# Output stages with a 512-column and a 256-column product per weight tile, and ScalarE's rounding of weights moved ahead

## The chip, the core and the metric

The kernel runs on one core of a Trainium2 chip. The metric is the device time of one execution in microseconds (us). TensorE (PE in the profile) multiplies matrices, VectorE (DVE) and ScalarE (ACT) work on rows of 128 partitions, GpSimd (POOL) does small odds and ends here, and SyncE (SP) issues most of the DMAs.

## The reference, cut to what matters

Two transformer-like blocks run one after the other on 256 tokens of width 2048, all in float32.

```
first block:  h = rms_norm(x); proj = h @ w_in            # 2048 x 8192
              y = [gated short convolution, causal attention], each normalised and gated
              x = x + y @ w_out                            # 2048 x 2048, first output stage
second block: modulation = silu(c) @ w_ada + b_ada        # 2048 x 12288, for c and c_ctx
              q, k, v, u = modulate(rms_norm(x)) @ w_in_2; k, v also of the context rows
              mix = [window attention with context keys, multi-scale pooling of u]
              x = x + g_a * (mix @ w_out_2)                # 2048 x 2048, second output stage
              x = x + g_m * (relu(modulate(rms_norm(x)) @ w_up)^2 @ w_down)   # 8192 wide
              rms_norm(x)
```

Products must be more exact than one pass in the reduced float32 format of TensorE gives, so each factor is split in a rounded part ("hi") and the rest ("lo"), and three products are summed: hi*hi, lo*hi and hi*lo. The fourth, lo*lo, is left out in both kernels.

## The kernel before, in words

**Units.** All large products are cut into units. A unit makes 128 output features for 256 tokens, from 16 weight tiles of 128x128. Its weights come in two halves of 8 tiles (128x1024 float32, 512 KB each). There are 248 units: 64 for the first projection, 16 for the first output stage (`U_OUT1`), 8 for keys and values (`U_KV`), 16 for queries and pooling (`U_Q`, `U_POOL`), 16 for the second output stage (`U_OUT2`), and 128 for the MLP in four groups of 16 up units and 16 down units.

**A half on its way.** SP loads it into one of 4 slots of `raw` (`weight`, L256), after VectorE has finished with what the slot held. ScalarE rounds it into `hi` (`split`, L757, the copy is recorded at L755) once the data are there and TensorE has used the half four places earlier (`w_used`). VectorE subtracts to get `lo` (`split`, L1090, recorded at L1088, since the helper `tt` has its call there) and signals `lo_done`. The four slots hold two units, so both engines prepare unit j+2 in the turn that belongs to unit j.

**TensorE.** `unit` (L402) calls `half_unit` twice. Each half waits for its own `lo_done`, and then issues three matmuls of 256 columns for each tile: hi by the activations' hi half (L396), lo by their hi half (L397), hi by their lo half (L398). All add into the first 256 columns of one PSUM bank, `G0` or `G1` by turns. A unit may begin when VectorE or ScalarE has emptied the unit two places earlier (`evac_done`). `pair_unit` (L413), which only the down units of the MLP use, issues two matmuls for each tile: hi by both activation halves at once, 512 columns into the full bank (L422), and lo by the hi half, 256 columns into the first half of the bank (L423). It waits for both weight halves before its first matmul. The bank then holds two parts, and VectorE must add both.

**The first output stage.** For unit j VectorE goes through `out_lap` (L1354): the lo part of unit j+2's first half, the addition of the bank to `resid` (L1362, recorded at L1088), two operations that make a tile of the modulated context (L1364, L1365), the lo part of unit j+2's second half, the lo part of the context tile (`actC`), and the addition of squares. ScalarE goes through `out_body` (L937): hi of the first half, hi of the context tile (which waits for L1365), the square of `resid`, and only then hi of the second half. One row of the modulation product (four groups of narrow matmuls, `ada_rows`, L438) stands between the two halves of each unit on TensorE; SP loads these rows (1 MB each) in its own order between the weights, and waits for an earlier row to be used first. The key and value units that follow read all 16 context tiles in order.

**The second output stage.** For unit j VectorE takes lo of the first half, multiplies the bank by the gate and adds it to `resid` (L1521), takes lo of the second half, makes the lo part of the MLP's input (L1525, which waits for ScalarE's hi part, L946) and adds squares. ScalarE takes hi of the first half, L946 (which waits for L1521), the square, and hi of the second half. The sum of squares gates the MLP's normalisation (`total_sums`, L467).

Of the kernel before, what the change touches and what calls it, by code (L numbers as in the profile page):

```python
# [7 lines left out]
ALU = mybir.AluOpType  # L8
# [7 lines left out]
T = 256  # L16
D = 2048
KT = D // P
# [6 lines left out]
UNITS_IN, UNITS_OUT = 64, 16  # L25
# [3 lines left out]
U_OUT1 = UNITS_IN  # L29
# [13 lines left out]
for _name, _n in (("gain1", 16), ("conv_w", 24), ("conv_gain", 8), ("attn_gain", 8), ("q_gain", 1), ("k_gain", 1),  # L43
# [13 lines left out]
    "act up": {"relu_done": 2, "nt_hi": 2, "hi_done": 4},  # L57
    "act down": {"hi_done": 4},
    "act last down": {"hi_done": 4, "sqs": 2, "sq_ready": 2},
    "dve w_out": {"seq": 4, "nt_ready": 4, "lo_done": 8, "nt": 4, "inC": 4, "sqs": 4, "sq_added": 4},  # L60
    "dve q": {"p_turned": 4, "p_copied2": 4, "rot": 2, "seq": 14, "rope_done": 2, "qr_ready": 2, "nt": 2, "inB": 2, "scores": 8, "negmax_ready": 2, "lo_done": 4, "tile": 2, "probs_scaled": 8},
    "dve w_out_2": {"lo_done": 8, "sqs": 4, "sq_added": 4, "x_hi": 4, "inA": 4},
    "dve up": {"relu_done": 2, "seq": 2, "lo_done": 4, "nt": 2, "inB": 2},
# [40 lines left out]
def program(nc, t_in, out):  # L104
    with ExitStack() as ctx:
# [275 lines left out]
        def _(pe):  # L381
# [20 lines left out]
            def unit(at, j, x, ready=None, ready_base=0, ada=None):  # L402
                half_unit(at, j, 0, x, ready, ready_base)
                if ada is not None:
                    if ada % KT == 0 and ada > 0:
                        ada_turn()
                    else:
                        ada_rows(ada)
                half_unit(at, j, 1, x, ready, ready_base)
                if ada is not None and ada % KT == 0 and ada > 0:  # L410
                    ada_rows(ada)
# [38 lines left out]
            def part_sums(n):  # L450

                pe.wait_ge(ada_taken, 4 * (n + 1))
                if n:
                    pe.wait_ge(part_added, n)
                for m in range(4):
                    x = pe.matmul(PART[:, m:m + 1], part[:, m * P:(m + 1) * P], ones[:, 0:1], start=(m == 0), stop=(m == 3),
                                  skip_group_check=True)
                x.then_inc(part_summed, 1)
# [89 lines left out]
                conv_body(HEADS + h)  # L548
            broadcast()
            for n in range(UNITS_OUT):  # L550
                unit(At(U_OUT1), n, actB, inB, ada=2 * KT + n)
                if n == 1:
                    part_sums(7)

            def total_sums(n):

# [146 lines left out]
            tile_values(1)  # L703
            tiles_of(bank, (7,)).then_inc(w_used, 1)
            tiles_of(bank, (8, 9), last=True).then_inc(w_used, 1)
            unit(at, 1, actB)
            with turn.lap(pe, (UNITS_OUT - 2) // 2, "pe w_out_2") as i:
                for j in range(2):
                    unit(At(U_OUT2 + 2, 2, i), j, actB)

            def up_unit(at, j):
                half_unit(at, j, 0, actU, extra=2)
# [34 lines left out]
        def _(act):  # L747
# [9 lines left out]
            def split(at, j, half=1):  # L757

                slot = (2 * j + half) % RING
                act.wait_ge(raw_full[slot], at.loads(j, half) * 16)  # L760
                act.wait_ge(w_used, at.unit(j, 1 + half, 2))
                copy(hi[:, slot], raw[:, slot]).then_inc(hi_done, 1)
                own(hi_done)
# [173 lines left out]
            def out_body(at, i, ctx_too):  # L937

                for j in range(4):
                    u = slice(i * 4 + j, i * 4 + j + 1) if isinstance(i, int) else bass.ds(i * 4 + j, 1)  # L940
                    split(at, j, 0)
                    if ctx_too:
                        high(actC[:, u, 0:T], t4[:, 3:4])
                    if not ctx_too:
                        evacuated(at, j)
                        act.activation(actU[:, u, 0:T], resid[:, u], ACT.Copy, scale=scale_m[:, u]).then_inc(x_hi, 1)  # L946
                        own(x_hi)
                    square(at, j, (sq[:, j % 2:j % 2 + 1], resid[:, u]))
                    split(at, j)

            with turn.lap(act, 4, "act w_out") as i:
                out_body(At(U_OUT1, 4, i), i, True)
# [118 lines left out]
        def _(dve):  # L1071
# [3 lines left out]
            def own(event):  # L1075

                dve.wait_ge(event, turn.next(event.name))
# [9 lines left out]
            def tt(dst, a, b, op):  # L1087
                return dve.tensor_tensor(dst, a, b, op)  # L1088

            def split(at, j, half=1):  # L1090

                slot = (2 * j + half) % RING
                dve.wait_ge(hi_done, at.unit(j, 5 + half, 2))
                tt(lo[:, slot], raw[:, slot], hi[:, slot], ALU.subtract).then_inc(lo_done, 1)
                own(lo_done)

            def summed(at, j):

                dve.wait_ge(w_used, at.unit(j, 2, 2))
                dve.wait_ge(evac_done, at.unit(j))  # L1100
                return G[j % 2][:, 0:T].rearrange("p (a t) -> p a t", a=1)

            def evacuated(at, j):
                dve.wait_ge(evac_done, at.unit(j, 1))
# [233 lines left out]
            def add_squares(s):  # L1338
                dve.wait_ge(sq_ready, turn.next("sqs") + 2 * HEADS + CONV_TILES)
                tt(sqsum[:], sqsum[:], sq[:, s], ALU.add).then_inc(sq_added, 1)  # L1340
                own(sq_added)
# [12 lines left out]
            def out_lap(at, i, first=False):  # L1354
                for j in range(4):
                    u = bass.ds(i * 4 + j, 1) if not isinstance(i, int) else slice(i * 4 + j, i * 4 + j + 1)
                    split(at, j, 0)
                    if j == 0 and first:
                        modulation_ready()
                    if j == 2 and first:  # L1360
                        part_add(7)
                    tt(resid[:, u], resid[:, u], summed(at, j), ALU.add).then_inc(evac_done, 1)  # L1362
                    dve.wait_ge(ctx_full[j], i * 16 + 16)
                    seq(dve.scalar_tensor_tensor(t4[:, 2:3], ctx_raw[:, j:j + 1], scale_a[:, 1, u], CTX_BC3, ALU.mult, ALU.mult))  # L1364
                    dve.tensor_scalar(t4[:, 3:4], t4[:, 2:3], adav[:, 1, u], None,  # L1365
                                      ALU.add).then_inc(nt_ready, 1)
                    own(nt_ready)
                    split(at, j)
                    low(actC[:, u, 0:T], actC[:, u, T:2 * T], t4[:, 3:4], inC)
                    add_squares(j % 2)  # L1370
# [142 lines left out]
            turn.base["inA"] = 2 * KT - turn.local.get("inA", 0)  # L1513


            with turn.lap(dve, 4, "dve w_out_2") as i:
                at = At(U_OUT2, 4, i)
                for j in range(4):
                    u = bass.ds(i * 4 + j, 1)
                    split(at, j, 0)  # L1520
                    dve.scalar_tensor_tensor(resid[:, u], summed(at, j), adav[:, 0, bass.ds(i * 4 + G_A + j, 1)],  # L1521
                                             resid[:, u], ALU.mult, ALU.add).then_inc(evac_done, 1)
                    split(at, j)
                    dve.wait_ge(x_hi, turn.next("x_hi"))
                    dve.scalar_tensor_tensor(actU[:, u, T + 2:], resid[:, u], scale_m[:, u], actU[:, u, 0:T], ALU.mult,  # L1525
                                             ALU.subtract).then_inc(inA, 1)
                    own(inA)
                    add_squares(j % 2)
            take_sums(ss[:, 8:10], SUMS[:, 0:2], add=False)
            dve.wait_ge(sum_taken, turn.value("sum"))  # L1530
            mean_square(ss[:, 8:10], D)
# [162 lines left out]
```

## Time and profile before

| what | us |
|---|---|
| three timed runs | 1774.19, 1772.69, 1773.1; median 1773.1 |
| the profiled execution, its own time | 1774.28 |
| its span in the profile | 1772.4 |
| busy: TensorE, VectorE, ScalarE | 1635.3, 1165.5, 768.3 |

The span runs from the first to the last instruction. 1.9 us of the execution's own time lie outside it. Busy times overlap, so they don't add up to the span. TensorE's matmuls are pipelined: in a row of the timeline the number after the start is how long one matmul takes from start to end, while the distance of two starts is what it costs in the stream.

### The profile page before, as it was taken

What the parts mean: (1) busy time and instruction counts of PE and PEld (TensorE: products, weight loads), DVE (VectorE), ACT (ScalarE), POOL (GpSimd) and SP (SyncE); (2) the same over time, 40 slices, a digit from 0 to 9 for tenths busy, and PEclk for the clock granted to TensorE, in tenths of its full rate; (3) what the DMA queues carried; (4) which work ended last, traced back from release to release, by engine and by line L of the source; (5) the groups of instructions that cost most, each with busy time, mean ns of one, the idle gap of its engine ahead of it and who ended that gap; (6) DMA issues with size and microseconds to landing.
All of it is one profiled execution on the core that took longest, in us unless ns stands there. A gap on an engine that the chain in (4) does not pass through costs nothing.

```text
span 1772.4 us, 33734 instructions
## 1 busy us (share of the span) xinstructions
PE 1635.3 (92%) x12254; PEld 1501.3 (85%) x12254; DVE 1165.5 (66%) x1798; ACT 768.3 (43%) x1067; POOL 32.0 (2%) x49
## 2 busy tenths in 40 slices
PE   3799999899969977998989889999999999999996
PEld 3799998799968867877878879989998999899985
DVE  4577776688885557576755566656665666566675
ACT  4344443344433334444434445434543454345542
POOL 0000000000000000000000010000000000000000
PEclk9899999899989999999999989999999999999998
DMA  7688787688848765762224445555555556555552
GB/s 298 245 277 293 282 289 243 233 318 334 318 169 323 277 242 186 296 254 92 76 84 152 147 151 184 185 188 189 180 188 189 188 179 187 189 184 186 180 190 92
DMA packets 88120, 374.74 MB, mean 211 GB/s; under 512 B 9985, under 2 KB 10513, under 8 KB 75233
## 3 DMA queue, kind: packets, MB, share of 16 engines
q1 hardware_dynamic: 82224, 335.97, 55.3%
q10 hardware_dynamic: 4608, 33.56, 5.2%
q0 software_dynamic: 1200, 4.02, 0.7%
q8 instruction: 60, 0.98, 0.2%
q14 instruction: 28, 0.22, 0.0%
HBM read 371.40 MB, written 2.10 MB: 211 GB/s over the span
## 4 chain that ended last, share of the span: by engine, by line
issue 71%; DVE 12%; PE 11%; ACT 5%; DVEq 1%; POOL 0%; ACTq 0%; POOLq 0%
DVE lo L1088 5%; ACT hi L755 2%; PE G L396 2%; PE G L397 2%; PE G L398 2%; PE ADA L438 1%; PE M L636 1%; ACT sq L934 1%; DVE sqsum L1088 1%; DVE blk L1088 1%; PE S L610 1%; DVE sm L1413 1%; PE S L623 1%; PE ADA L650 1%; ACT actA L946 0%
## 5 line engine op out<-in xcount | busy, mean ns | idle before, releaser
L1088 DVE TENSOR_TENSOR lo<-raw,hi 128x1024 fp32r<-128x1024 f32 x496 | 607.8, 1225 | 326.1 <-ACT hi L755 316.0
L755 ACT ACTIVATE hi<-raw 128x1024 fp32r<-128x1024 f32 x496 | 526.1, 1061 | 488.1 <-PE G L398 276.4
L396 PE MATMUL G<-actA,hi 128*128 128x256 f32 (+1 forms) x2368 | 685.2, 289 | 20.1 <-DVE actA L1088 19.5
L397 PE MATMUL G<-actA,lo 128*128 128x256 f32 (+1 forms) x2368 | 672.5, 284 | 0.0
L398 PE MATMUL G<-actA,hi 128*128 128x256 f32 x2368 | 672.2, 284 | 0.0
L396 PEld LDWEIGHTS G<-actA,hi 128*128 128x128 f32 x2368 | 452.8, 191 | 54.5 <-issue 39.7
L397 PEld LDWEIGHTS G<-actA,lo 128*128 128x128 f32 x2368 | 452.4, 191 | 0.4
L398 PEld LDWEIGHTS G<-actA,hi 128*128 128x128 f32 x2368 | 451.6, 191 | 0.0
L422 PE MATMUL G<-actB,hi 128*128 128x512 f32 x1024 | 355.2, 391 | 0.0
L423 PE MATMUL G<-actB,lo 128*128 128x256 f32 x1024 | 287.2, 281 | 0.0
L422 PEld LDWEIGHTS G<-actB,hi 128*128 128x128 f32 x1024 | 191.6, 187 | 41.4
L423 PEld LDWEIGHTS G<-actB,lo 128*128 128x128 f32 x1024 | 194.2, 190 | 0.0
L396 PE MATMUL G<-actB,hi 128*128 128x256 f32 x496 | 147.2, 297 | 13.0 <-DVE resid L1521 5.3
L397 PE MATMUL G<-actB,lo 128*128 128x256 f32 x496 | 141.8, 286 | 0.0
L398 PE MATMUL G<-actB,hi 128*128 128x256 f32 x496 | 141.7, 286 | 0.0
L396 PEld LDWEIGHTS G<-actB,hi 128*128 128x128 f32 x496 | 96.6, 195 | 33.0 <-DVE lo L1088 10.8
L773 ACT ACTIVATE W<-G 128x256 f32<-128x256 f32 x80 | 30.7, 384 | 167.2 <-PE G L398 110.0
L397 PEld LDWEIGHTS G<-actB,lo 128*128 128x128 f32 x496 | 96.7, 195 | 0.1
L398 PEld LDWEIGHTS G<-actB,hi 128*128 128x128 f32 x496 | 96.5, 195 | 0.0
L438 PE MATMUL ADA<-ada_raw,cpad 128*32 128x512 f32 x512 | 69.1, 622 | 9.9 <-DVE adav L1088 6.7
L1180 DVE SCALAR_TENSOR_TENSOR part<-ada_raw,cpad,part 128x512 f32<-128x512 f32 x88 | 66.2, 752 | 7.2 <-DMA ada_raw<-w_ada_dram 4.2
L1088 DVE TENSOR_TENSOR acc<-acc,G 128x256 f32 x96 | 40.4, 421 | 33.4 <-PE G L423 31.8
(186 smaller groups left out, 1102.1 us busy)
## 6 DMA issues: line engine op xcount, KB each, us to landing
raw<-stream_dram SPq DMA_DIRECT2D x496, 512.0 KB, 3.5
ada_raw<-w_ada_dram SPq DMA_DIRECT2D x64, 1024.0 KB, 6.7
ada_raw<-w_ada_dram ACTq DMA_DIRECT2D x32, 1024.0 KB, 6.4
x_tok<-x_tok_dram SPq DMA_DIRECT2D x1, 2048.0 KB, 8.2
resid<-xT_dram SPq DMA_DIRECT2D x1, 2048.0 KB, 11.7
ctx_tok<-ctx_tok_dram SPq DMA_DIRECT2D x1, 2048.0 KB, 18.5
W<-ctxT_dram POOLq DMA_DIRECT2D x16, 128.0 KB, 5.5
out_dram<-resid SPq DMA_DIRECT2D x4, 512.0 KB, 2.6
```

Source lines behind the costliest of these rows:

```text
L396: pe.matmul(wide, hi[:, slot, cols], x[:, k, 0:T + extra], start=(k == 0), stop=False, skip_group_check=True)
L397: pe.matmul(wide, lo[:, slot, cols], x[:, k, 0:T + extra], start=False, stop=False, skip_group_check=True)
L398: m = pe.matmul(bank, hi[:, slot, cols], x[:, k, T + extra:2 * T + extra], start=False, stop=(k == KT - 1), skip_group_check=True)
L422: pe.matmul(bank[:], hi[:, slot, cols], x[:, k, :], start=(k == 0), stop=False, skip_group_check=True)
L423: m = pe.matmul(bank[:, 0:T], lo[:, slot, cols], x[:, k, 0:T], start=False, stop=(k == KT - 1), skip_group_check=True)
L438: m = pe.matmul(ADA[32 * g:32 * g + 32, :], cpad[:, 4 * (k % 4) + g, 6 - 2 * (k // 4):38 - 2 * (k // 4)], ada_raw[:, slot, g, :], start=(k ...
L610: pe.matmul(bank[:, 0:T], q, kT[rows, s, :], start=True, stop=False, skip_group_check=True)
L623: m = pe.transpose(S[c][:, k * P:(k + 1) * P], probs[:, c, k * P:(k + 1) * P], ident[:])
L755: return act.activation(dst, src, ACT.Copy)
L773: act.activation(dst, G[j % 2][:, 0:T], func).then_inc(evac_done, 1)
L1088: return dve.tensor_tensor(dst, a, b, op)
L1180: seq(dve.scalar_tensor_tensor(part[:], w, c, part[:], ALU.mult, ALU.add))
```

## The change

Both output stages use `pair_unit`, so each tile has a 512-column and a 256-column matmul in place of three of 256 columns (the very first unit of the second stage keeps the three). VectorE adds the second half of the bank with an operation of its own. In the first stage the row of the modulation product goes ahead of the unit, and the last row behind the stage. In `out_body` ScalarE rounds both weight halves of unit j+2 before anything else of the turn. VectorE's loop of the second stage is written out, 16 turns without a hardware loop.

```diff
--- before.py
+++ after.py
@@ -57,7 +57,7 @@
     "act up": {"relu_done": 2, "nt_hi": 2, "hi_done": 4},
     "act down": {"hi_done": 4},
     "act last down": {"hi_done": 4, "sqs": 2, "sq_ready": 2},
-    "dve w_out": {"seq": 4, "nt_ready": 4, "lo_done": 8, "nt": 4, "inC": 4, "sqs": 4, "sq_added": 4},
+    "dve w_out": {"seq": 8, "nt_ready": 4, "lo_done": 8, "nt": 4, "inC": 4, "sqs": 4, "sq_added": 4},
     "dve q": {"p_turned": 4, "p_copied2": 4, "rot": 2, "seq": 14, "rope_done": 2, "qr_ready": 2, "nt": 2, "inB": 2, "scores": 8, "negmax_ready": 2, "lo_done": 4, "tile": 2, "probs_scaled": 8},
     "dve w_out_2": {"lo_done": 8, "sqs": 4, "sq_added": 4, "x_hi": 4, "inA": 4},
     "dve up": {"relu_done": 2, "seq": 2, "lo_done": 4, "nt": 2, "inB": 2},
@@ -548,9 +548,14 @@
                 conv_body(HEADS + h)
             broadcast()
             for n in range(UNITS_OUT):
-                unit(At(U_OUT1), n, actB, inB, ada=2 * KT + n)
+                if n == 0:
+                    ada_turn()
+                else:
+                    ada_rows(2 * KT + n - 1)
+                pair_unit(At(U_OUT1), n, actB, inB)
                 if n == 1:
                     part_sums(7)
+            ada_rows(3 * KT - 1)
 
             def total_sums(n):
 
@@ -703,10 +708,10 @@
             tile_values(1)
             tiles_of(bank, (7,)).then_inc(w_used, 1)
             tiles_of(bank, (8, 9), last=True).then_inc(w_used, 1)
-            unit(at, 1, actB)
+            pair_unit(at, 1, actB)
             with turn.lap(pe, (UNITS_OUT - 2) // 2, "pe w_out_2") as i:
                 for j in range(2):
-                    unit(At(U_OUT2 + 2, 2, i), j, actB)
+                    pair_unit(At(U_OUT2 + 2, 2, i), j, actB)
 
             def up_unit(at, j):
                 half_unit(at, j, 0, actU, extra=2)
@@ -939,6 +944,7 @@
                 for j in range(4):
                     u = slice(i * 4 + j, i * 4 + j + 1) if isinstance(i, int) else bass.ds(i * 4 + j, 1)
                     split(at, j, 0)
+                    split(at, j)
                     if ctx_too:
                         high(actC[:, u, 0:T], t4[:, 3:4])
                     if not ctx_too:
@@ -946,7 +952,6 @@
                         act.activation(actU[:, u, 0:T], resid[:, u], ACT.Copy, scale=scale_m[:, u]).then_inc(x_hi, 1)
                         own(x_hi)
                     square(at, j, (sq[:, j % 2:j % 2 + 1], resid[:, u]))
-                    split(at, j)
 
             with turn.lap(act, 4, "act w_out") as i:
                 out_body(At(U_OUT1, 4, i), i, True)
@@ -1100,6 +1105,9 @@
                 dve.wait_ge(evac_done, at.unit(j))
                 return G[j % 2][:, 0:T].rearrange("p (a t) -> p a t", a=1)
 
+            def second(j):
+                return G[j % 2][:, T:2 * T].rearrange("p (a t) -> p a t", a=1)
+
             def evacuated(at, j):
                 dve.wait_ge(evac_done, at.unit(j, 1))
 
@@ -1359,7 +1367,8 @@
                         modulation_ready()
                     if j == 2 and first:
                         part_add(7)
-                    tt(resid[:, u], resid[:, u], summed(at, j), ALU.add).then_inc(evac_done, 1)
+                    seq(tt(resid[:, u], resid[:, u], summed(at, j), ALU.add))
+                    tt(resid[:, u], resid[:, u], second(j), ALU.add).then_inc(evac_done, 1)
                     dve.wait_ge(ctx_full[j], i * 16 + 16)
                     seq(dve.scalar_tensor_tensor(t4[:, 2:3], ctx_raw[:, j:j + 1], scale_a[:, 1, u], CTX_BC3, ALU.mult, ALU.mult))
                     dve.tensor_scalar(t4[:, 3:4], t4[:, 2:3], adav[:, 1, u], None,
@@ -1513,19 +1522,22 @@
             turn.base["inA"] = 2 * KT - turn.local.get("inA", 0)
 
 
-            with turn.lap(dve, 4, "dve w_out_2") as i:
-                at = At(U_OUT2, 4, i)
-                for j in range(4):
-                    u = bass.ds(i * 4 + j, 1)
-                    split(at, j, 0)
-                    dve.scalar_tensor_tensor(resid[:, u], summed(at, j), adav[:, 0, bass.ds(i * 4 + G_A + j, 1)],
-                                             resid[:, u], ALU.mult, ALU.add).then_inc(evac_done, 1)
-                    split(at, j)
-                    dve.wait_ge(x_hi, turn.next("x_hi"))
-                    dve.scalar_tensor_tensor(actU[:, u, T + 2:], resid[:, u], scale_m[:, u], actU[:, u, 0:T], ALU.mult,
-                                             ALU.subtract).then_inc(inA, 1)
-                    own(inA)
-                    add_squares(j % 2)
+            at = At(U_OUT2)
+            for j in range(UNITS_OUT):
+                u = slice(j, j + 1)
+                gate = adav[:, 0, G_A + j:G_A + j + 1]
+                split(at, j, 0)
+                if j == 0:
+                    dve.scalar_tensor_tensor(resid[:, u], summed(at, j), gate, resid[:, u], ALU.mult, ALU.add).then_inc(evac_done, 1)
+                else:
+                    seq(dve.scalar_tensor_tensor(resid[:, u], summed(at, j), gate, resid[:, u], ALU.mult, ALU.add))
+                    dve.scalar_tensor_tensor(resid[:, u], second(j), gate, resid[:, u], ALU.mult, ALU.add).then_inc(evac_done, 1)
+                split(at, j)
+                dve.wait_ge(x_hi, j + 1)
+                dve.scalar_tensor_tensor(actU[:, u, T + 2:], resid[:, u], scale_m[:, j:j + 1], actU[:, u, 0:T], ALU.mult,
+                                         ALU.subtract).then_inc(inA, 1)
+                own(inA)
+                add_squares(j % 2)
             take_sums(ss[:, 8:10], SUMS[:, 0:2], add=False)
             dve.wait_ge(sum_taken, turn.value("sum"))
             mean_square(ss[:, 8:10], D)
```

## Rows read from the trace of the kernel before

**Rows 1.** The page, busy time, share of the span and instructions of each engine.
```profile
PE 1635.3 (92%) x12254; PEld 1501.3 (85%) x12254; DVE 1165.5 (66%) x1798; ACT 768.3 (43%) x1067; POOL 32.0 (2%) x49
```

**Rows 2.** Windows: stretch, length, busy (count) by engine, clock, DMA share, GB/s.
```profile
660.00:695.00 35.00, 26.27 (x198) 25.75 (x198) 31.03 (x60) 16.05 (x28) 3.83 (x6) 0.89 0.57 206
...
916.00:1025.00 109.00, 96.17 (x750) 91.09 (x749) 59.84 (x80) 47.02 (x62) 0.00 (x0) 1.00 0.45 145
```

**Rows 3.** Waits, second output stage: who waited for whom, us, times, longest.
```profile
DVE lo L1088 <- ACT hi L755: 33.8, 16, 2.5
```

**Rows 4.** Timeline of VectorE, second output stage: start, us, what, [idle before <-releaser].
```profile
961.35 0.48 DVE L1521 SCALAR_TENSOR_TENSOR resid<-G,adav,resid 128x256 f32 x1 [0.26 <-DVE lo L1088]
964.01 1.23 DVE L1088 TENSOR_TENSOR lo<-raw,hi 128x1024 fp32r<-128x1024 f32 x1 [2.18 <-ACT hi L755]
965.59 0.49 DVE L1525 SCALAR_TENSOR_TENSOR actA<-resid,scale_m,actA  x1 [0.35 <-DVE lo L1088]
966.20 0.43 DVE L1088 TENSOR_TENSOR sqsum<-sqsum,sq 128x256 f32<-128x256 f32 x1
...
968.23 0.48 DVE L1521 SCALAR_TENSOR_TENSOR resid<-G,adav,resid 128x256 f32 x1 [0.26 <-DVE lo L1088]
```

**Rows 5.** Timeline of ScalarE, the same turn.
```profile
961.92 0.51 ACT L946 ACTIVATE actA<-resid,scale_m 128x256 fp32r<-128x256 f32 x1 [3.74 <-DVE resid L1521]
...
962.91 2.15 ACT L755 ACTIVATE hi<-raw 128x1024 fp32r<-128x1024 f32 x2
```

**Rows 6.** Timeline of VectorE, first output stage, one turn and the last addition.
```profile
585.22 1.23 DVE L1088 TENSOR_TENSOR lo<-raw,hi 128x1024 fp32r<-128x1024 f32 x1 [2.35 <-ACT hi L755]
...
590.17 0.35 DVE L1365 TENSOR_SCALAR t<-t,adav 128x256 f32<-128x256 f32 x1 [0.15 <-DVE t L1364]
592.88 1.23 DVE L1088 TENSOR_TENSOR lo<-raw,hi 128x1024 fp32r<-128x1024 f32 x1 [2.35 <-ACT hi L755]
...
652.28 0.42 DVE L1088 TENSOR_TENSOR resid<-resid,G 128x256 f32 x1 [0.26 <-DVE lo L1088]
```

**Rows 7.** Timeline of ScalarE in the first of these turns.
```profile
590.65 0.42 ACT L755 ACTIVATE actC<-t 128x256 f32 x1 [4.37 <-DVE t L1365]
591.34 0.42 ACT L934 ACTIVATE sq<-resid 128x256 f32 x1 [0.27 <-ACT actC L755]
```

**Rows 8.** Timeline of TensorE, first output stage and the sum of squares after it.
```profile
534.85 0.58 PE L396 MATMUL G<-actB,hi 128*128 128x256 f32 x1
...
538.87 1.07 PE L438 MATMUL ADA<-ada_raw,cpad 128*32 128x512 f32 x8
...
542.84 0.95 PE L456 MATMUL S<-ones,part 128*128 128x1 f32 x8
...
546.69 1.07 PE L438 MATMUL ADA<-ada_raw,cpad 128*32 128x512 f32 x8
...
609.14 1.07 PE L438 MATMUL ADA<-ada_raw,cpad 128*32 128x512 f32 x8
...
641.56 1.07 PE L438 MATMUL ADA<-ada_raw,cpad 128*32 128x512 f32 x8
...
658.65 0.85 PE L467 MATMUL S<-ones,sqsum 128*128 128x1 f32 x4
```

**Rows 9.** Timeline of TensorE, second output stage and the sum of squares after it.
```profile
916.66 0.28 PE L396 MATMUL G<-actB,hi 128*128 128x256 f32 x1
...
918.46 0.28 PE L396 MATMUL G<-actB,hi 128*128 128x256 f32 x1
...
1029.92 1.01 PE L467 MATMUL S<-ones,sqsum 128*128 128x1 f32 x4 [8.33 <-DVE sqsum L1088]
```

**Rows 10.** Timeline of VectorE, first down stage of the MLP, additions 13 units apart.
```profile
1140.16 0.88 DVE L1088 TENSOR_TENSOR acc<-acc,G 128x256 f32 x2 [0.68 <-PE G L423]
...
1212.26 0.88 DVE L1088 TENSOR_TENSOR acc<-acc,G 128x256 f32 x2 [0.66 <-PE G L423]
```

**Rows 11.** Windows: early in the first output stage, columns as in Rows 2.
```profile
535.00:542.00 7.00, 7.00 (x49) 6.03 (x50) 3.30 (x4) 2.67 (x4) 0.54 (x1) 0.85 1.01 407
```

## The prediction

> **What bounds the kernel now.** I read the busy line first: TensorE is busy 92% of the span [rows 1], which would leave little but its own work. Then I cut the span into stages with the windows. In the second output stage the stretch from 916 to 1025 shows 750 matmuls in 109.0 us [rows 2]. Matmuls of 256 columns start 0.120 us apart when nothing holds them: 15 of them lie between the starts at 916.66 and 918.46, 1.80 us [rows 9]. 750 x 0.120 is 90 us, so some 19 us of this stage are stalls, though TensorE looks busy, because the ends of matmuls are modelled.
>
> The waits tell what stalls it. VectorE waited 33.8 us in 16 pieces for ScalarE's hi copy [rows 3]. The timelines of both engines show the ring. VectorE adds the bank (961.35), ScalarE can then make the MLP's hi tile (961.92, 0.51 us), squares, and rounds the second half at 962.91 (two copies, 2.15 us); VectorE's lo starts only at 964.01, after 2.18 us idle [rows 4, 5]. From one L1521 to the next are 968.23 - 961.35 = 6.88 us [rows 4], and nothing of that is a wait for TensorE. A unit of 48 matmuls takes 48 x 0.120 = 5.76 us. So the exchange between VectorE and ScalarE sets the pace, and TensorE follows it.
>
> The first output stage has the same ring, hidden for a while. Its turn is 592.88 - 585.22 = 7.66 us, of which VectorE idles 2.36 us, from the end of L1365 at 590.52 to 592.88 [rows 6], while ScalarE makes the context tile, squares (591.34) and rounds [rows 7]. TensorE runs at (609.14 - 546.69) / 9 = 6.94 us per unit [rows 8]: 5.76 us of matmuls and 1.18 us for the row of the modulation product. VectorE therefore falls behind. TensorE's last row is at 641.56 (then 2.9 us of the last half), but VectorE's last addition is at 652.28 [rows 6, 8]. The key and value units need VectorE's 16th context tile, and the sum of squares is taken only at 658.65 [rows 8]. What follows is VectorE's chain of normalised tiles (31.03 us busy of 35 from 660 to 695) [rows 2], which starts from that sum. So what the first stage gains at 658.65 goes straight to the end.
>
> **The change part by part.**
>
> *Two matmuls for three.* The price is in the down stage, where units have this form and nothing else holds them: 13 units between the additions at 1140.16 and 1212.26 are 72.10 us, 5.55 us per unit [rows 10]. Against 5.76 us that is 0.21 us less, for 31 units 6.5 us if TensorE set the pace. The Trainium skill ("TensorE: Matmul & The Clock Gate", section "Back-to-back issue gap") gives for single matmuls columns / 2.4 plus 2.5 ns each. By that rule a dropped matmul would save 2.5 ns, an estimate of 1.2 us over 496 tiles, and the total below would be about 5 us less. The trace disagrees with it on 256 columns (0.120 us against 0.109 us by the rule), and the stage with just these shapes decides.
>
> *ScalarE's order.* This is the large part. hi of the second half now waits only for TensorE's end of unit j. VectorE's addition waits for the same event. So from that end on, ScalarE rounds (1.06 us, half of the 2.15 us pair) [rows 5] while VectorE adds twice, and lo of the second half can start at once. The 2.18 and 2.36 us idle stretches go. In exchange, the tile copy and the square come behind both roundings. In the second stage after L1521's successor ScalarE needs 0.51 + 0.42 us, while VectorE is busy for 1.23 us with lo, so L1525 still finds its tile. In the first stage the context tile (0.42) and the square (0.27 gap and 0.42) [rows 7] end about 1.2 us after L1365, beside the same lo.
>
> *VectorE's second addition.* It costs 0.48 us (L1521) or 0.42 us [rows 4, 6], and 0.12 us of hand-over (966.20 less the end of L1525 at 966.08) [rows 4]. VectorE's own turn in the second stage is 6.88 - 2.18 = 4.70, plus 0.60 for the addition and 0.12 for the new hand-over before lo: 5.42 us. TensorE's is 5.55. In the first stage it is 7.66 - 2.36 + 0.42 + 0.24 = 5.96 us against 5.55 + 1.18 = 6.73. TensorE sets the pace in both, by 0.13 and 0.77 us. The written-out loop can only shorten the 0.26 and 0.35 us gaps before L1521 and L1525 [rows 4]; I count nothing for it.
>
> *Waiting for both halves.* Seen from the end of unit j, VectorE finishes lo of unit j+2's second half after 0.1 + 0.48 + 0.12 + 0.48 + 0.12 + 1.23 = 2.5 us (second stage), or about 3.5 us with the context operations (first stage). TensorE asks for it after unit j+1, at 5.55 or 6.73 us. That leaves 3 us, so the wait costs nothing. If the cover were gone, the price would be at most the half, 2.9 us per unit.
>
> *The moved rows.* ada_turn now precedes the first unit; TensorE stands waiting for data there, and the first unit's end depends on VectorE's tiles. The row before unit 1 waits for the same modulation result, so unit 1 still opens at 534.85. SP's next row load waits for a row used at the start of unit j+1 and not in the middle of unit j, about 4 us later. The weight loads of unit j+4 are queued behind it, with about two units (13 us) until they are rounded. Traffic rises: two halves, a row and a context tile are 2.23 MB in 6.73 us, 331 GB/s. The DMA engines moved 407 GB/s where they were full [rows 11], so the loads fit, at a share near 0.85. Bounds: 0, or, if only some 300 GB/s came through, 7.4 us per unit and 9 us lost. I take 0, since the full-share row is the nearest.
>
> *The sum, first stage.* Unit 1 opens at 534.85. Its first half takes 538.87 - 534.85 = 4.0 us where 24 x 0.120 are 2.9 [rows 8], with the granted clock at 0.85 of full speed in that stretch [rows 11], part at the lower level of 1.2 GHz after the idle stretch; I keep that 1.05 us. End 541.45; partial sums 0.95 (L456) to 542.40; row 1.18; unit 2 to 549.1. Then 13 units of 6.73 are 87.5, to 636.6. Last row, 637.8. Key/value unit 0 of 5.76, to 643.6; context tile 15 is ready by then. The sum of squares comes at 643.6 in place of 658.65: 15.1 us.
>
> *Second stage.* Unit 1 opens at 916.66 as now. 15 units of 5.55 are 83.2, to 999.85. VectorE's last turn from there: 2.5 us to the end of lo, 0.35 + 0.49 for L1525, 0.12 + 0.43 for the squares, 1003.8. The sum of squares comes at 1003.9 in place of 1029.92 [rows 9]: 26.0 us. In between and behind, the stages are paced by their own chains and shift as they are.
>
> Total 41.1 us. The profiled execution took 1774.28, which gives 1733.2. The median of the timed runs is 1.2 below it, so I predict 1732.
>
> **The rivals.**
>
> *One stage does not reach TensorE's pace.* VectorE's margin in the second stage is only 0.13 us; in the first, the DMA demand is near what the engines carry. At 7.4 us per unit the first stage gains 13 x 0.67 = 9 us less: about 1741. At 6.0 us per unit the second gains 7 us less: 1739. For it: small margins. Against it: the down stage keeps 5.55 us with two additions, and the full-share row.
>
> *The first stage's gain is absorbed.* If the key/value stage waited for its weights or modulation rows rather than for the sum, only the second stage would count: 1774.3 - 26 - 1.2, about 1747. For it: SP's order is in lockstep and the loads come later relative to use. Against it: VectorE was 89% busy there, in its own chain [rows 2].
>
> *The ring stays, and the change is slower.* Place: ScalarE's second rounding in out_body. If the event it waits for (end of unit j) still came after VectorE was otherwise free, the ring would hold 6.88 + 0.60 and about 7.9 + 0.54 us, while a unit of TensorE could no longer start on its first half. Price 15 x 0.60 + 15 x 0.54 = 17 us: 1790. It decides when lo of the second half starts later than 1.2 us after the second addition. Against it: in the down stage the same order of two roundings runs without a stall of TensorE.
>
> *Only the matmul count matters*: 6.5 us, 1767. Against it are the idle rows.
>
> **How the numbers follow.** Forecast 0.76, one stage short 0.12, absorbed 0.06, only the count 0.02, ring stays and slower 0.04. The forecast's own range is 1728 to 1737. To hold 8 in 10 and the price of a short stage I give 1726 to 1744. A measurement of this kernel can tell 0.2%, 3.5 us, from no change. All cases but the ring are faster by more: faster 0.95, same 0.01, slower 0.04.
>
> **What would show it.** In the second stage additions at G 5.55 us apart, lo of the second half without a wait for ScalarE's hi after the second addition, and L467 near 1029.9 - 41 = 989 us. In the first, rows of L438 6.73 us apart without DMA waits, L467 near 643.6. A granted clock below 1.00 in these windows, waits of L438 for a DMA, or additions further apart than VectorE's own sum would prove a step wrong.

## The result

The changed kernel takes 1732.39 us (median of five runs, 1731.10 to 1735.69), the kernel before, run beside it, 1772.69 (1772.04 to 1774.19). The ratio is 0.9775 with a 95% interval of 0.9762 to 0.9788: 40 us or 2.3% faster. The forecast was 1732, in a range of 1726 to 1744.

The profiled execution of the changed kernel is the slowest of its five, 1735.69 us with a span of 1733.8, so the traces show 38.6 us where the medians show 40.3.

The page of the changed kernel, its busy line, answers to [rows 1]:

```profile
PE 1620.1 (93%) x11758; PEld 1467.5 (85%) x11758; DVE 1179.1 (68%) x1829; ACT 768.5 (44%) x1067; POOL 32.1 (2%) x49
```

496 matmuls are gone and VectorE has 31 instructions more. TensorE's share barely moved; the 40 us can't be seen here.

The windows of the changed kernel over the key/value stage and the second output stage, with the columns of [rows 2]:

```profile
640.00:675.00 35.00, 31.26 (x248) 30.22 (x244) 28.82 (x56) 17.05 (x28) 3.83 (x6) 0.96 0.59 205
...
900.00:985.00 85.00, 84.66 (x481) 73.46 (x482) 65.77 (x94) 47.67 (x64) 0.00 (x0) 1.00 0.60 180
```

The second row now has 85.00 us with 84.66 of TensorE. The waits of that stage answer to [rows 3]:

```profile
ACT hi L760 <- PE G L423: 35.8, 29, 2.0
...
DVE lo L1093 <- ACT hi L760: 10.4, 16, 0.9
...
DVE resid L1533 <- PE G L423: 5.8, 14, 0.4
```

VectorE's wait for ScalarE fell from 33.8 to 10.4 us. ScalarE's own waits are now for TensorE (35.8 us), and VectorE waits for TensorE too, where it adds the bank (5.8 us). One turn of VectorE in the timeline, against [rows 4]:

```profile
924.59 0.48 DVE L1533 SCALAR_TENSOR_TENSOR resid<-G,adav,resid 128x256 f32<-128x256 f32 x1 [0.40 <-PE G L423]
925.11 0.48 DVE L1534 SCALAR_TENSOR_TENSOR resid<-G,adav,resid 128x256 f32<-128x256 f32 x1
925.71 1.22 DVE L1093 TENSOR_TENSOR lo<-raw,hi 128x1024 fp32r<-128x1024 f32 x1
926.97 0.48 DVE L1537 SCALAR_TENSOR_TENSOR actA<-resid,scale_m,actA 128x256 fp32r<-128x256 f32 x1
927.49 0.42 DVE L1093 TENSOR_TENSOR sqsum<-sqsum,sq 128x256 f32<-128x256 f32 x1
928.61 1.23 DVE L1093 TENSOR_TENSOR lo<-raw,hi 128x1024 fp32r<-128x1024 f32 x1 [0.69 <-ACT hi L760]
930.25 0.48 DVE L1533 SCALAR_TENSOR_TENSOR resid<-G,adav,resid 128x256 f32<-128x256 f32 x1 [0.42 <-PE G L423]
```

And ScalarE in the same turn, against [rows 5]:

```profile
924.61 1.06 ACT L760 ACTIVATE hi<-raw 128x1024 fp32r<-128x1024 f32 x1 [1.75 <-PE G L423]
925.71 0.51 ACT L952 ACTIVATE actA<-resid,scale_m 128x256 fp32r<-128x256 f32 x1
926.25 0.42 ACT L939 ACTIVATE sq<-resid 128x256 f32<-128x256 f32 x1
927.44 1.06 ACT L760 ACTIVATE hi<-raw 128x1024 fp32r<-128x1024 f32 x1 [0.77 <-PE G L423]
```

The two engines start together at 924.6: ScalarE rounds for 1.06 us while VectorE adds twice, and lo follows at 925.71 with no wait put down to ScalarE. The turn is 930.25 - 924.59 = 5.66 us, where it was 6.88. VectorE is idle twice in it. The 0.40 us are ended by TensorE. The 0.69 us are ended by ScalarE's rounding at 927.44, and that one had itself waited 0.77 us for TensorE. So both idle times go back to TensorE. TensorE's own marks, against [rows 8, 9]:

```profile
534.50 1.93 PE L438 MATMUL ADA<-ada_raw,cpad 128*32 128x512 f32 x8 [3.63 <-DVE adav L1093]
...
544.11 1.06 PE L438 MATMUL ADA<-ada_raw,cpad 128*32 128x512 f32 x8
...
632.47 1.07 PE L438 MATMUL ADA<-ada_raw,cpad 128*32 128x512 f32 x8
...
646.12 0.50 PE L467 MATMUL S<-ones,sqsum 128*128 128x1 f32 x4
...
901.72 0.40 PE L422 MATMUL G<-actB,hi 128*128 128x512 f32 x1
...
990.15 0.61 PE L467 MATMUL S<-ones,sqsum 128*128 128x1 f32 x4 [0.59 <-DVE sqsum L1093]
```

Rows of the modulation product are (632.47 - 544.11) / 13 = 6.80 us apart, without one wait for a DMA. The first sum of squares comes at 646.12, the second at 990.15.

### The profile page after: what moved, and what is told of

Its sections match the earlier page's. It is cut to its first block, busy times and chain, and to the rows that moved or that the text cites. A ratio compares the mean times of both kernels' runs of the same rounds, so it can differ in the third digit from the quotient of the medians.

```text
span 1733.8 us, 32628 instructions
## 1 busy us (share of the span) xinstructions
PE 1620.1 (93%) x11758; PEld 1467.5 (85%) x11758; DVE 1179.1 (68%) x1829; ACT 768.5 (44%) x1067; POOL 32.1 (2%) x49
## 4 chain that ended last, share of the span: by engine, by line
issue 72%; PE 20%; DVE 6%; ACT 1%; POOL 0%; POOLq 0%; DVEq 0%; ACTq 0%
PE G L422 7%; PE G L423 3%; PE ADA L438 2%; PE G L396 2%; PE G L398 2%; PE G L397 2%; DVE lo L1093 1%; PE M L641 1%; DVE blk L1093 1%; DVE sm L1422 1%; PE S L628 1%; ACT hi L760 1%; PE S L615 1%; PE ADA L655 1%; DVE blk L1435 0%
## 5 line engine op out<-in xcount | busy, mean ns | idle before, releaser
L422 PE MATMUL G<-actB,hi 128*128 128x512 f32 x1520 | 535.5, 396 | 3.2 <-DVE actB L1093 3.2
L422 PEld LDWEIGHTS G<-actB,hi 128*128 128x128 f32 x1520 | 286.2, 188 | 81.8 <-issue 13.4
L438 PE MATMUL ADA<-ada_raw,cpad 128*32 128x512 f32 x512 | 68.7, 618 | 6.9 <-DVE adav L1093 6.7
L1093 DVE TENSOR_TENSOR actB<-t,actB 128x256 f32 (+1 forms) x88 | 37.4, 425 | 20.7 <-DVE t L1093 18.8
L351 POOL TENSOR_TENSOR rr<-ms,neg_half 128x4 f32<-128x4 f32 x15 | 15.2, 1013 | 1474.9 <-DVE ms L1128 1474.9
L473 PE MATMUL M<-W,ones 128*128 128x256 f32 x28 | 11.3, 492 | 33.0 <-DVE W L1123 33.0
L1059 ACT ACTIVATE t<-W,sm 128x256 f32<-128x256 f32 x64 | 32.7, 511 | 16.8 <-ACT hi L760 11.9
L1557 DVE TENSOR_REDUCE sm<-G 128x1 f32<-128x2 f32 x64 | 10.2, 159 | 38.3 <-PE G L398 38.1
L473 PEld LDWEIGHTS M<-W,ones 128*128 128x128 f32 x28 | 5.0, 223 | 33.6 <-issue 17.0
```

Source lines behind the costliest of these rows:

```text
L422: pe.matmul(bank[:], hi[:, slot, cols], x[:, k, :], start=(k == 0), stop=False, skip_group_check=True)
L438: m = pe.matmul(ADA[32 * g:32 * g + 32, :], cpad[:, 4 * (k % 4) + g, 6 - 2 * (k // 4):38 - 2 * (k // 4)], ada_raw[:, slot, g, :], start=(k ...
L1059: act.activation(t4[:, j], scaled[:, j], ACT.Relu, bias=sm[:, 40 + j:41 + j]).then_inc(relu_done, 1)
```

## The experiments

Two explanations were set against each other. Theory "ring": the gain is the broken exchange between VectorE and ScalarE; TensorE sets the pace afterwards, and the two matmuls in place of three are only a small part. Rival "matmuls": the two matmuls in place of three bring the gain. All ratios are against the kernel before, run beside each; its medians lay between 1774.4 and 1774.9 there, some 2 us above those of the result, so ratios are compared, and 0.001 is 1.8 us. The two columns on the right are from the profile of each kernel, in us. The first is counted from the row of L438 just ahead of unit 1 to the first sum of squares, the second from there to the second sum.

| kernel | median us | ratio, 95% | that row to first sum | first to second sum |
|---|---|---|---|---|
| before | (beside each) | 1 | 125.7 | 371.3 |
| changed | 1732.4 | 0.9775 (0.9762 to 0.9788) | 111.6 | 344.0 |
| only ScalarE's order | 1737.4 | 0.9798 (0.9779 to 0.9817) | 113.4 | 346.9 |
| changed, old order | 1774.3 | 0.9997 (0.9986 to 1.0007) | 130.4 | 367.0 |
| first stage only | 1758.0 | 0.9908 (0.9892 to 0.9925) | 111.2 | 368.4 |
| second stage only | 1748.9 | 0.9855 (0.9839 to 0.9872) | 125.6 | 344.6 |
| one addition | 1732.4 | 0.9761 (0.9744 to 0.9778) | 111.7 | 342.4 |
| three more additions | 1748.8 | 0.9856 (0.9841 to 0.9871) | 117.6 | 349.0 |
| clearing moved | 1729.4 | 0.9748 (0.9735 to 0.9762) | 111.1 | 343.6 |
| loop kept | 1734.6 | 0.9776 (0.9763 to 0.9790) | 111.5 | 342.9 |
| old order, waits by halves | 1775.2 | 1.0000 (0.9991 to 1.0010) | 130.8 | 364.6 |
| clearing moved, loop kept | 1731.8 | 0.9762 (0.9748 to 0.9776) | 112.4 | 345.4 |

### Only ScalarE's order

```diff
--- before
+++ only the order
                     split(at, j, 0)
+                    split(at, j)
                     if ctx_too:
...
                     square(at, j, (sq[:, j % 2:j % 2 + 1], resid[:, u]))
-                    split(at, j)
```

> The kernel before, with ScalarE's rounding of both weight halves moved to the front of its turn in both output stages and nothing else. Theory 'ring' (the gain is the broken exchange between VectorE and ScalarE): TensorE sets the pace with 48 matmuls of 256 columns, 5.76 us per unit in the second stage and 6.94 us in the first, so 41.1 - 31 x 0.21 = 34.6 us less than before, about 1738 us, and VectorE no longer idles 2.2 us ahead of lo of the second half. Rival 'matmuls' (the two wider matmuls bring the gain): 0 to 2 us less, 1771 to 1773.

One line moved gives 0.9798, 36 of the 40 us. In the timeline of VectorE in the second stage TensorE has become the releaser, with 48 matmuls per unit still in place:

```profile
955.00 0.48 DVE L1521 SCALAR_TENSOR_TENSOR resid<-G,adav,resid 128x256 f32 x1 [0.71 <-PE G L398]
955.95 1.23 DVE L1088 TENSOR_TENSOR lo<-raw,hi 128x1024 fp32r<-128x1024 f32 x1 [0.46 <-ACT hi L755]
```

lo of the second half starts 0.47 us after the addition ends, where 2.18 us lay between [rows 4]. "Matmuls" had 1771 to 1773 us for this kernel and falls.

### The changed kernel with the old order

The same line moved back, in the changed kernel.

> The changed kernel with ScalarE's old order (second half rounded last in the turn); two matmuls per tile and two additions stay. Theory 'ring': the ring holds, longer by an addition: 6.9 + 0.6 = 7.5 us per unit in the second stage, 7.9 + 0.54 = 8.5 in the first, and a unit can't start on its first half: 17 us slower than before, about 1790 us. Rival 'matmuls': 6.5 us faster than before, 1766. Third way: the second addition is hidden and only the first stage's late end counts, within 3 us of before.

It is as fast as before (0.9997), so the numbers of both "ring" and "matmuls" missed. The third way's number came, but not for its reason: the ring is there in both stages. VectorE in the second stage:

```profile
957.40 0.48 DVE L1533 SCALAR_TENSOR_TENSOR resid<-G,adav,resid 128x256 f32<-128x256 f32 x1
957.92 0.48 DVE L1534 SCALAR_TENSOR_TENSOR resid<-G,adav,resid 128x256 f32<-128x256 f32 x1
960.59 1.22 DVE L1093 TENSOR_TENSOR lo<-raw,hi 128x1024 fp32r<-128x1024 f32 x1 [2.18 <-ACT hi L760]
...
964.08 0.48 DVE L1533 SCALAR_TENSOR_TENSOR resid<-G,adav,resid 128x256 f32<-128x256 f32 x1
```

The 2.18 us wait is back to the hundredth, and the turn is 6.68 us. I had put it at 6.9 + 0.6. Without the wait VectorE's turn is 4.50 us with two additions, where it was 4.70 with one: the addition adds 0.52, and the shorter hand-overs, where this loop is written out, take 0.72 off, which I had counted as nothing. No run has the old order together with the loop. In the first stage, where the loop stayed, VectorE's turns are 8.1 to 8.7 us, near the 8.5 expected. Between the two sums this kernel is 4.3 us better than before, up to the first sum 4.7 us worse. They cancel. So without the order the rest of the change is worth nothing in the timed runs.

### Waits by halves in the old order

```diff
-                pe.wait_ge(lo_done, at.unit(j, 2, 2))
+                pe.wait_ge(lo_done, at.unit(j, 1 if out else 2, 2))
...
+                    if out and k == 8:
+                        pe.wait_ge(lo_done, at.unit(j, 2, 2))
```

> The changed kernel with ScalarE's old order, as in the run before of that kind (1774.3 us, the ring stayed), and with the output stages' units waiting for each weight half apart, as three-matmul units do. It shows whether the wait for both halves costs anything once the ring is there. Theory 'the ring alone sets the pace': VectorE's additions stay 6.7 us apart and the time stays within 3 us of 1774. Rival 'the whole-unit wait is part of the pace': 5 us or more faster, 1769 or less.

The ratio is 1.0000, against 0.9997 with the whole wait. VectorE's turn is again 6.68 us:

```profile
950.86 0.48 DVE L1536 SCALAR_TENSOR_TENSOR resid<-G,adav,resid 128x256 f32<-128x256 f32 x1
...
957.54 0.48 DVE L1536 SCALAR_TENSOR_TENSOR resid<-G,adav,resid 128x256 f32<-128x256 f32 x1
```

With the old order the wait for both halves costs nothing that the timed runs can tell, since TensorE is not what sets the pace there. With the new order it was not tried.

### One stage at a time

Each kernel takes TensorE's part, VectorE's additions, ScalarE's order (by `if ctx_too`) and, for the second, the written-out loop, for its own stage.

> The change in the first output stage alone, the second as before. The sum gives the first stage 15.1 us; the two profiles give 14 us up to the first sum of squares and 2 to 3 us in the stages that follow it. So 1756 to 1758 us. If the first stage's gain were absorbed behind it (rival), 1770 or more, and the second-stage kernel would have nearly all of the 40 us.

> The change in the second output stage alone, the first as before. The sum gives 26.0 us, the two profiles 24.5 us: 1747 to 1748 us. The gains of this and of the first-stage kernel should add up to the 40 us of the whole change within 2 us, if the stages are independent, as the theory has it; if they share a cause (a clock that stays up, say), the two would add up to less or more by over 3 us.

0.9908 and 0.9855 are 16.3 and 25.7 us, together 42, against 40 for the whole. Nothing of the first stage's gain is absorbed later. The 2 us between the sum and the whole lie within the intervals. The spans of the three profiles leave more, 16.3 + 27.5 against 38.6 us, and the traces show 3 of those 5 us: 1.6 in the second stage, and 1.5 behind the second sum (see "GpSimd's clearing moved"). The second stage alone has its additions 5.55 us apart:

```profile
943.86 0.48 DVE L1530 SCALAR_TENSOR_TENSOR resid<-G,adav,resid 128x256 f32<-128x256 f32 x1 [0.36 <-PE G L423]
...
949.41 0.48 DVE L1530 SCALAR_TENSOR_TENSOR resid<-G,adav,resid 128x256 f32<-128x256 f32 x1 [0.36 <-PE G L423]
```

That is the 5.55 forecast, where the changed kernel has 5.66 with the same instructions.

### VectorE's margin

The first kernel drops the second addition, so it leaves out the product of the weights' hi part with the activations' lo part. The second repeats, three times for each unit and stage, `seq(tt(t4[:, 0:1], resid[:, u], second(j), ALU.add))` ahead of it, an addition into an unused tile.

> The changed kernel without VectorE's second addition in both output stages; it leaves out the product of the weights' hi part with the activations' lo part there. Theory 'TensorE sets the pace': the addition lies beside TensorE's 5.65 us per unit, so 0 to 1 us less, 1731 to 1733. Rival 'VectorE still sets the pace' (by the prediction's own sum it had only 0.13 us of margin in the second stage): 15 x 0.5 in the second stage and some in the first, 1722 to 1726.

> The changed kernel with three more additions of the bank's second half into an unused tile per unit, in both stages, each 0.42 us and some 0.1 us of hand-over. VectorE waited about 1.1 us of its 5.65 us turn in the second stage and about 1.2 of 6.8 in the first. Theory 'TensorE sets the pace with about 1.1 us of margin': 1.5 us more work is 0.4 us over in each turn, 5 to 12 us slower than the changed kernel, 1738 to 1744. Rival 'no margin, as the prediction's 5.42 us had it': 1.4 x 15 + 0.9 x 15 = 34 us slower, 1766. Rival 'the margin is larger, the work hides': 1732.

Without the addition the ratio is 0.9761, within the interval of 0.9775: the addition is hidden. Its profile is 1.6 us shorter between the two sums, but TensorE's matmuls stand closer there (0.346 us per tile, see the last experiment), as they do in two kernels that have the addition. With three more it is 0.9856, 14 us slower, over the 5 to 12 expected. Its profile, in which the two intervals cost 6.0 and 4.9 us, is of its fastest run (1742.2, mean granted clock 0.976). The other three took 1748.2 to 1749.9 at 0.972, and no trace shows where their 6 to 8 us lie. VectorE in the second stage then never waits:

```profile
940.66 0.48 DVE L1535 SCALAR_TENSOR_TENSOR resid<-G,adav,resid 128x256 f32<-128x256 f32 x1
941.18 1.33 DVE L1093 TENSOR_TENSOR t<-resid,G 128x256 f32<-128x256 f32 x3
942.55 0.48 DVE L1538 SCALAR_TENSOR_TENSOR resid<-G,adav,resid 128x256 f32<-128x256 f32 x1
...
946.54 0.48 DVE L1535 SCALAR_TENSOR_TENSOR resid<-G,adav,resid 128x256 f32<-128x256 f32 x1
```

Its turn is 5.88 us; without the three (942.55 - 941.18 = 1.37 us) it would be 4.51. So VectorE's own work in the changed kernel is 4.5 us against TensorE's 5.66, a margin of 1.1 us and not of 0.13. The 4.50 of the old order say the same.

### The loop kept

Four turns written out, then three laps of four in a hardware loop.

> The changed kernel with VectorE's second output stage as a hardware loop again (three laps of four units behind four written out). The hand-overs in the loop were 0.26 and 0.35 us and written out 0.04, some 0.7 us per turn. Theory 'TensorE sets the pace with 1.1 us of margin': nothing changes, 1732. Rival 'the written-out loop is what makes VectorE fit': VectorE's turn of 5.4 us and its waits for ScalarE add up to more than 5.65, 3 to 8 us slower, 1735 to 1740.

The ratio is 0.9776 against 0.9775: no difference. VectorE's turn in the loop, in a place where TensorE was ready for it, so that the gaps ahead of the two additions (0.46 and 0.44 us) are about its own hand-over:

```profile
946.76 0.48 DVE L1533 SCALAR_TENSOR_TENSOR resid<-G,adav,resid 128x256 f32 x1 [0.46 <-DVE lo L1093]
...
952.08 0.48 DVE L1533 SCALAR_TENSOR_TENSOR resid<-G,adav,resid 128x256 f32 x1 [0.44 <-PE G L423]
```

It is 5.32 us, near the 5.42 that the prediction had worked out from the loop before. Here the margin to TensorE's 5.55 is nearly as thin as forecast, and it is enough. Writing the loop out adds nothing that the timed runs can tell once the order is right.

### GpSimd's clearing moved

```diff
                 power(14)
+                pool.wait_ge(bc_ready, 14)
                 pool.memset(acc, 0.0).then_inc(acc_zero, 1)
```

> The changed kernel with GpSimd's clearing of acc moved behind the broadcast of the MLP's norm. Where it is now, VectorE's two small products that this broadcast needs take 3.5 us instead of 0.48 beside it, and TensorE waits 2.34 us for them. If the clearing slows them: 2.3 us less, about 1730, and the products take 0.5 us. If they are slow for another reason: no change. TensorE's program is that of the changed kernel, so its spacing of 0.353 us per tile in the second stage should show again if it belongs to the program, and 0.346 if it changes from one execution to the next.

The clearing is a GpSimd instruction that sets a tile of the MLP to zero. In the changed kernel it starts just ahead of VectorE's two products of 128x128 that the broadcast needs:

```profile
992.39 3.51 POOL L376 MEMSET acc<- 128x4096 f32 x1
992.52 3.52 DVE L1123 TENSOR_SCALAR W<-ident,rr 128x128 f32<-128x128 f32 x2 [0.83 <-POOL rr L351]
```

With the clearing behind the broadcast:

```profile
989.62 0.48 DVE L1124 TENSOR_SCALAR W<-ident,rr 128x128 f32<-128x128 f32 x2 [0.83 <-POOL rr L351]
```

3.52 us became 0.48, and TensorE's broadcast starts 3.4 us after the sum of squares and not 5.9. The Trainium skill ("SBUF — State Buffer", section "SBUF: two separate sides") says that VectorE's instructions in a two-port mode and GpSimd's share a pair of ports, and that whichever starts first holds it as an exclusive lock to its end. The trace agrees in time: the clearing ends at 995.90, the products at 996.04. Which mode the products ran in it does not show.

The ratio 0.9748 (0.9735 to 0.9762) against 0.9775 (0.9762 to 0.9788) is 4.8 us, and the intervals touch. From the second sum to the end the profiles have 743.7 us in the changed kernel and 739.4 here. The earlier broadcast is 2.5 of these 4.3 us. Most of the rest lies right behind it. These are the windows of 3.4 us that begin 0.3 us after the broadcast, in the changed kernel, in this one, and in the kernel with one addition (columns as in [rows 2], the clock third from the end):

```profile
996.40:999.80 3.40, 3.40 (x16) 3.26 (x15) 2.16 (x5) 0.00 (x0) 0.00 (x0) 0.50 0.00 0
```

```profile
991.00:994.40 3.40, 3.40 (x30) 3.37 (x29) 2.56 (x5) 1.34 (x2) 3.06 (x1) 1.00 0.01 1
```

```profile
994.60:998.00 3.40, 3.40 (x29) 3.35 (x28) 2.44 (x5) 0.26 (x1) 0.00 (x0) 1.00 0.00 0
```

In the changed kernel TensorE's granted clock was 0.50 there, its lower level of 1.2 GHz, after a wait of 2.34 us for the products, and it got through 16 matmuls where the two others did 30 and 29. The kernel with one addition has the early clearing and the same wait, and kept the full clock. So the clearing alone does not decide this part. The kernel with the clearing moved has the lowest time and ratio of all.

### The best version in sight, and the spacing of matmuls

> The best version in sight: the changed kernel with the clearing of acc moved behind the broadcast (3.0 us less when alone) and VectorE's second stage as a loop, where TensorE ran at 0.346 us per tile and not 0.353 (1.7 us over 15 units). If both hold together: 1728 us. If TensorE's spacing comes from something else in the program, it is 0.353 here and the time 1729 to 1731.

> The changed kernel once more, unchanged, for one profile. If the spacing of 0.353 us per tile in the second output stage belongs to the program, it shows again; if it changes from one execution to the next, it can be 0.346.

Clearing moved and loop kept is 0.9762, or 1731.8 us where 1728 was expected if both gains held, and 1729 to 1731 otherwise: no better than clearing moved alone. The spacing, which is the distance of two 512-column starts, stayed at 0.353 us per tile. A second profile of the changed kernel (1735.1 us) shows 0.353 as well:

```profile
924.74 0.40 PE L422 MATMUL G<-actB,hi 128*128 128x512 f32 x1
...
925.10 0.40 PE L422 MATMUL G<-actB,hi 128*128 128x512 f32 x1
...
925.45 0.40 PE L422 MATMUL G<-actB,hi 128*128 128x512 f32 x1
```

The kernel with the loop kept has 0.346 in the same place:

```profile
924.88 0.39 PE L422 MATMUL G<-actB,hi 128*128 128x512 f32 x1
...
925.22 0.40 PE L422 MATMUL G<-actB,hi 128*128 128x512 f32 x1
...
925.57 0.39 PE L422 MATMUL G<-actB,hi 128*128 128x512 f32 x1
```

So the spacing came again in a second execution of the same kernel, and it changes between kernels that issue the same matmuls there. What sets it stays open.

## Why the prediction was right

The mechanism held. That the median (1732.39) lies within half a microsecond of 1732 is luck. The profiled execution was to take 1733.2 us by the forecast and took 1735.7. Both stages gave about 1 us less than forecast, the stretch between them 2.4 us more, and 2.7 us were lost ahead of unit 1 and behind the second sum.

**The ring sets the pace.** Shown: the reordered line alone gives 36 of 40 us, and taking it away from the changed kernel gives all of them back.

**Two matmuls for three.** I had 6.5 us. The changed kernel against the reordered one is 0.9775 against 0.9798, some 4 us with wide intervals; in the traces the two intervals differ by 1.8 and 2.9, 4.7 us together. The estimate of 1.2 us by the rule on single matmuls of the Trainium skill ("TensorE: Matmul & The Clock Gate", section "Back-to-back issue gap") is too low. Of the missing 1.8 us, 15 x 0.11 = 1.6 are the wider spacing in the second stage.

**First stage.** Forecast 15.1 us. The trace has 125.7 - 111.6 = 14.1. The turn was 6.80, not 6.73: 13 x 0.07 is the 0.9 us. The loads stayed hidden at 326 GB/s and a share of 0.88:

```profile
550.00:610.00 60.00, 60.00 (x355) 44.21 (x354) 43.62 (x73) 26.03 (x36) 4.29 (x8) 1.00 0.88 326
```

331 GB/s and a share near 0.85 were forecast; the bound of 7.4 us per unit did not come.

**Second stage.** Forecast 26.0 us from the opening of unit 1. The trace has (1029.92 - 916.66) - (990.15 - 901.72) = 24.8; 15 units of 5.66 instead of 5.55 are 1.6 us less.

**Between the stages** I had counted nothing. From the first sum to unit 1 it was 258.0 us [rows 8, 9] and is 901.72 - 646.12 = 255.6. The kernel with only the first stage changed has 255.2 there, the one with only the second 257.8, so this gain comes with the first stage's change. Its cause is open. Before, TensorE stood idle just ahead of the first sum:

```profile
657.84 0.58 PE L396 MATMUL G<-actC,hi 128*128 128x256 f32 x1 [5.54 <-DVE actC L1088]
```

In the changed kernel the row before the sum has no such wait, and the mean granted clock between the sum and unit 1 is 0.95 and not 0.94. But the old order with waits by halves, which has the late sum too, needs only 256.6 us there, so the idle time is not the whole of it.

**Ahead and behind**, the profiled execution lost 1.5 us before unit 1 and 1.2 us behind the second sum. 14.1 + 24.8 + 2.4 - 1.5 - 1.2 = 38.6. The 1.2 us are, within 0.2, the 14 matmuls fewer in the stretch at the lower clock level shown above (14 x 0.12 = 1.7 us), less a broadcast that came 0.3 us sooner after its sum. The 1.5 us are no effect of the change: that row of L438 begins between 531.6 and 534.8 us in the profiles of the other kernels, whose program ahead of it is the same.

**VectorE's margin** is the term that was mis-sized. I gave its turn 5.42 us and the written-out loop nothing. In the loop it is 5.32, written out 4.5. The 6.88 us that I worked from was also one turn and not the mean: the sixteen additions before are 7.0 us apart on average, with three gaps of 7.3. The error did not touch the time, as TensorE was the slower one either way. It did touch the slower rival, priced at 1790: the changed kernel with the old order takes 1774. In the second stage its turn is 6.68 us where 7.5 were priced, because the written-out loop pays for the second addition. Up to the first sum it is 4.7 us slower where 15 x 0.54 = 8.1 were priced, with turns near the forecast. The rival's deciding point held: with lo released by ScalarE 2.18 us after the last addition, the ring stays.

## What to carry to other kernels

When an engine is busy by the profile but its units come further apart than its instructions add up to, look for two other engines that hand work to each other in every turn, and ask of each step whether it needs the other's result or only stands behind it in program order. Work that depends on an early event should be queued ahead of work that depends on a late one. Price a rearrangement by each engine's own turn, with its hand-overs, against the slowest; and before calling an added operation hidden or costly, count what else in the same edit shortens that engine's turn.

## What the runs showed of the hardware

- Two VectorE products of 128x128 float32 took 3.52 us beside a GpSimd clearing of 128x4096 (3.51 us), and 0.48 without it.
- The same pair of matmuls (512 and 256 columns) started every 0.346 us in three kernels' second stage and every 0.353 us in three others', steadily, at a granted clock of 1.00. It was the same in two executions of one kernel.
- With the same two products and the same wait of 2.34 us ahead of the broadcast, TensorE's granted clock was 0.50 for 3.4 us behind it in the changed kernel and 1.00 in the kernel with one addition.
- In VectorE's hardware loop the gaps ahead of L1521 and L1525 (here L1533 and L1537) were 0.26 to 0.46 us; written out, the gap ahead of L1537 was 0.04.
